# A hybrid attention layer: the output stage's first two row tiles prepared inside the last differential slots, the variance moved off VectorE, and the first loads put between stores

## What is computed

```python
h = _rmsnorm(x, g_pre[layer])
proj = h @ w_in[layer]
...
y_sb = _stick_breaking(...).reshape(b, s_len, SB_WIDTH) * jax.nn.silu(sb_g)
# differential attention: two softmaxes per head over key chunks <= the query's chunk
p = jax.nn.softmax(jnp.where(allowed, sc, -jnp.inf), axis=-1)
a = p[:, :, 0] - lam * p[:, :, 1]
o = einsum('bhqk,bkhe->bqhe', a, v)
y_df = _rmsnorm(o, g_subln) * (1.0 - lambda_init) * jax.nn.silu(df_g)
...
y_m = softmax(mq @ mk) @ mv * jax.nn.silu(m_g)
y = jnp.concatenate([y_sb, y_df, y_m], axis=-1) @ w_out[layer]
x = x + _rmsnorm(y, g_post[layer])
```

## Time and profile before

| | us |
|---|---|
| median of 3 runs (lowest, highest) | 1971.78 (1969.61, 1973.33) |
| the profiled execution, its own time | 1971.71 |
| its span in the trace | 1969.9 |
| PE busy | 1837.9 (93%) |
| DVE busy | 1299.6 (66%) |
| ACT busy | 1076.0 (55%) |
| POOL busy | 606.9 (31%) |

### The profile page before, as it was taken

One profiled execution on the slowest core, in us unless ns is written; L12 is line 12 of the kernel. 1 busy time (PEld: TensorE's weight loads), 2 busy tenths in 40 slices (PEclk: granted clock), 3 DMA queues, 4 the chain that ended last, 5 costly groups with the idle time before them and its releaser, 6 DMA issues.

```text
span 1969.9 us, 34242 instructions
## 1 busy us (share of the span) xinstructions
PE 1837.9 (93%) x11552; PEld 1549.6 (79%) x11552; DVE 1299.6 (66%) x2657; ACT 1076.0 (55%) x2378; POOL 606.9 (31%) x545
## 2 busy tenths in 40 slices
PE   6999999899999999999999999999788999979998
PEld 6999999778787878787777787777566666658886
DVE  7704888577777777777777764344677878753554
ACT  6421112266666666666666753343588998951221
POOL 0000000044444444444444431112246666650000
PEclk9999999899999999999999899998699999999999
DMA  7423213100000101010101013324601432025542
GB/s 223 107 70 112 69 64 118 49 6 13 20 19 13 24 8 25 7 27 5 27 5 27 6 38 115 106 90 133 134 1 40 82 76 44 9 97 203 176 144 86
DMA packets 121841, 129.10 MB, mean 66 GB/s; under 512 B 81937, under 2 KB 94993, under 8 KB 120465
## 3 DMA queue, kind: packets, MB, share of 16 engines
q1 hardware_dynamic: 121312, 126.29, 22.4%
q0 software_dynamic: 432, 1.57, 0.3%
HBM read 85.89 MB, written 41.94 MB: 65 GB/s over the span
## 4 chain that ended last, share of the span: by engine, by line
PE 70%; DVE 14%; issue 6%; ACT 6%; DMA 2%; POOL 1%; SPq 1%; DVEq 0%; ACTq 0%; POOLq 0%
PE ps L685 9%; PE ps L671 6%; PE ps L639 6%; PE ps L640 5%; PE ps L641 5%; DVE small L1541 4%; PE ps L622 3%; PE ps L624 3%; PE ps L623 3%; PE ps L908 3%; PE ps L909 3%; PE ps L910 3%; PE ps L659 3%; PE ps L660 3%; PE ps L859 2%
## 5 line engine op out<-in xcount | busy, mean ns | idle before, releaser
L1664 POOL TENSOR_TENSOR ring_r<-ring,sp_hi 128x512 fp32r<-128x512 f32 (+1 forms) x320 | 359.6, 1124 | 437.5 <-DVE sp_hi L1423 437.5
L685 PEld LDWEIGHTS ps<-v,ring 128*128 128x128 f32 x2176 | 290.0, 196 | 62.8 <-issue 27.4
L685 PE MATMUL ps<-v,ring 128*128 128x65 f32 x2176 | 292.5, 275 | 20.2 <-ACT ring L1070 12.4
L1058 ACT ACTIVATE ring<-ps 128x512 f32<-128x512 f32 (+1 forms) x320 | 170.5, 533 | 218.7 <-PE ps L660 127.6
L1420 DVE SCALAR_TENSOR_TENSOR ring<-ring,ps 128x512 f32<-128x512 f32 (+1 forms) x320 | 192.1, 600 | 44.4 <-ACT ring L1063 41.8
L622 PE MATMUL ps<-w_hl,ht_hi 128*128 128x256 f32 x768 | 213.6, 278 | 0.7 <-DVE w_hl L1268 0.6
L1690 POOL TENSOR_TENSOR p<-p 128x1024 f32<-128x1024 f32 (+4 forms) x96 | 164.7, 1727 | 159.3 <-ACT p L1180 159.0
L623 PE MATMUL ps<-w_hl,ht_hi 128*128 128x256 f32 x768 | 213.3, 278 | 0.0
L624 PE MATMUL ps<-w_hl,ht_lo 128*128 128x256 f32 x768 | 213.3, 278 | 0.0
L639 PE MATMUL ps<-ht_hi,w_hl 128*128 128x512 f32 x448 | 199.6, 446 | 5.2 <-DVE sb_s L1450 4.2
L1541 DVE TENSOR_REDUCE small<-ps 128x1 f32<-128x1024 f32 (+4 forms) x192 | 168.7, 906 | 46.6 <-PE ps L817 26.1
(11 more groups left out here) (202 smaller groups left out, 3897.7 us busy)
## 6 DMA issues: line engine op xcount, KB each, us to landing
xb<-in_x SPq DMA_DIRECT2D x16, 512.0 KB, 3.9
gate_scr<-ring SPq DMA_DIRECT2D x64, 128.0 KB, 1.8
cs<-rot_scr SPq DMA_DIRECT2D x32, 256.0 KB, 3.9
gb<-gate_scr SPq DMA_DIRECT2D x16, 512.0 KB, 3.8
yb<-y_scr SPq DMA_DIRECT2D x16, 512.0 KB, 4.7
xr<-in_x SPq DMA_DIRECT2D x16, 512.0 KB, 4.3
out_y<-ob SPq DMA_DIRECT2D x16, 512.0 KB, 2.9
w_raw<-in_w_narrow SPq DMA_DIRECT2D x15, 512.0 KB, 3.7
```

The lines of the kernel that those rows point to most:

```text
L685: mm = pe.matmul(ps[:, 4 + i % 2, j * (HD + 1):(j + 1) * (HD + 1)], ring[:, 4 + i % 2, j * P:(j + 1) * P], v1[:, kb, :], start=True, stop= ...
L1664: nc.gpsimd.tensor_tensor(ring_r[:, i % 4, j0 * P:], ring[:, i % 4, j0 * P:], sp_hi[:, i % 4, j0 * P:].bitcast(F32), ALU.subtract).then_in ...
```

## The change

Four things are changed.

1. **Variance without VectorE.** `df_variance` keeps only the sum. ScalarE takes Ln of sum/64 + eps directly (scale and a bias column `eps_col`, one more memset at the start), and GpSimd makes the variance for its Newton step itself, as the first instruction of `df_norm`. VectorE's sum now waits until GpSimd and ScalarE have read the sum of the block before.
2. **First two row tiles inside the last slots.** Gates of tiles 0 to 3 are loaded in slot 29, the rows in slot 31. VectorE gates tiles 0, 1 and 2 at the end of slots 32, 33 and 35; TensorE transposes tiles 0 and 1 in slots 33 and 34; `out_hi` and `out_lo` of both stand at the end of slots 33 and 34. The products follow directly behind the loop.
3. **Residual rows and `g_post`** are loaded in slot 35, ahead of the last block's store.
4. **First differential loads between stores.** Head 0's values are loaded in slot 27, and the four parts of its queries and keys in slots 28, 29, 30 and 31, each behind that slot's store of the memory stage.

```diff
-                    load_qk(0)
-                    load_df_v(0)
+                if 3 <= slot - X_SLOT[-1] < 7:
+                    load_qk(0, ((0, 2 * DQ), (0, 0), (1, 2 * DQ), (2, 0))[slot - X_SLOT[-1] - 3])
...
-                if s == N_SL:
+                if s == N_SL - 3:
+                    for i in range(4):
+                        load_gate(i)
+                if s == N_SL - 1:
                     for i in range(4):
                         load_y(i)
+                if s == N_SL + 3:
+                    sp.wait_ge(df_z, N_SL * UNITS)
+                    for u in range(2):
+                        load_xr(u)
+                    sp.wait_ge(df_o, N_SL * N_GR)
+                    sp.dma_start(gpost_b[:], g_post.broadcast_to((P, D))).then_inc(gpost_in, 16)
...
+                if s == N_SL + 1:
+                    pe.wait_ge(df_e, N_SL * UNITS)
+                if s in (N_SL + 1, N_SL + 2):
+                    out_transposes(s - N_SL - 1)
                 df_scores(s, 5)
...
-            pe.wait_ge(df_ob, N_SL // 2)
-            out_transposes(0)
-            out_transposes(1)
             pe.wait_ge(wo_lo_ok, DC)
             for i in range(SB):
+                if i == 1:
+                    pe.wait_ge(df_ob, N_SL // 2)
                 out_products(i)
...
-                rsqrt_of(df_tmp(4, 4), df_tmp(8, 4), df_tmp(12, 4), df_var, s // 2 + 1, df_ln, df_y0)
+                b = s // 2
+                act.wait_ge(df_ss, b + 1)
+                if b:
+                    act.wait_ge(df_nr, 4 * b)
+                nc.scalar.activation(df_tmp(8, 4), df_tmp(0, 4), ACT.Ln, scale=1.0 / HD, bias=eps_col).then_inc(df_ln, 1)
+                act.wait_ge(df_ln, b + 1)
+                nc.scalar.activation(df_tmp(12, 4), df_tmp(8, 4), ACT.Exp, scale=-0.5).then_inc(df_y0, 1)
...
                 df_exp(s, 5)
+                if s in (N_SL + 1, N_SL + 2):
+                    out_hi(s - N_SL - 1)
...
                 dve.wait_ge(df_sq, b + 1)
+                if b:
+                    dve.wait_ge(df_var, b)
+                    dve.wait_ge(df_ln, b)
                 nc.vector.tensor_reduce(ss, osq[:], AXX, ALU.add).then_inc(df_ss, 1)
-                dve.wait_ge(df_ss, b + 1)
-                if b:
-                    dve.wait_ge(df_nr, 4 * b)
-                nc.vector.tensor_scalar(var, ss, 1.0 / HD, EPS, ALU.mult, ALU.add).then_inc(df_var, 1)
...
                 df_rows(s - 4)
+                if s in (N_SL, N_SL + 1, N_SL + 3):
+                    out_gate((N_SL, N_SL + 1, N_SL + 3).index(s))
+                if s in (N_SL + 1, N_SL + 2):
+                    out_lo(s - N_SL - 1)
...
+                pool.wait_ge(df_ss, b + 1)
+                nc.gpsimd.tensor_scalar(var, df_tmp(0, 4), 1.0 / HD, EPS, ALU.mult, ALU.add).then_inc(df_var, 1)
+                pool.wait_ge(df_var, b + 1)
                 pool.wait_ge(df_y0, b + 1)
-                pool.wait_ge(df_var, b + 1)
```

More of the change, by code:

```diff
@@ L447, in store_qk, with load_qk @@
                 sp.dma_start(qk_scr[h, 1, :, cols], lo_tmp[:, f % 2, :].bitcast(F32)).then_inc(qk_out[f % 2], 16)
-            def load_qk(h):
+            def load_qk(h, only=None):
                 u, half = h % 2, S // 2
                 for part, dst, row, first in ((0, df_k, 2 * DQ, 0), (0, df_q, 0, half), (1, df_k, 2 * DQ, half), (2, df_q, 0, 0)):
+                    if only not in (None, (part, row)):
+                        continue
                     cols = slice(first, first + half)
@@ L481, in _ @@
                         store_qk(f)
+                if slot == X_SLOT[-1] + 2:
+                    load_df_v(0)
                 if slot == X_SLOT[-1] + 3:
@@ L496, in _, with load_xr @@
             load_qk(1)
+            def load_xr(i):
+                if i >= 2:
+                    sp.wait_ge(o_fin, i - 1)
+                sp.dma_start(xr[:, i % 2, :], x[OUT_ROWS[i] * P:(OUT_ROWS[i] + 1) * P, :]).then_inc(o_xr[i % 2], 16)
             def load_wo(k):
@@ L501, in load_wo, with load_gate @@
                 sp.dma_start(w_raw[:, (k % 2) * D:(k % 2 + 1) * D], w_out[k * P:(k + 1) * P, :]).then_inc(wo_in[k % 2], 16)
+            def load_gate(i):
+                if i == 0:
+                    sp.wait_ge(df_z, (DF_H - 1) * 8 * UNITS)
+                row = OUT_ROWS[i]
+                sp.dma_start(gb[:, i % 4, :], gate_scr[row * P:(row + 1) * P, :]).then_inc(o_in[i % 4], 16)
             def load_y(i):
@@ L553, in store @@
                 sp.dma_start(out[OUT_ROWS[i] * P:(OUT_ROWS[i] + 1) * P, :], ob[:, i % 2, :]).then_inc(o_out[i % 2], 16)
-            for u in range(2):
-                load_xr(u)
             for i in range(SB):
@@ L911, in out_products @@
                     mm.then_inc(o_ps, 1)
-            pe.wait_ge(df_ob, N_SL // 2)
-            out_transposes(0)
-            out_transposes(1)
+            for s in range(N_SL + 4):
+                df_scores(s, 0)
+                df_scores(s, 1)
+                df_turn(s - 2, 0)
+                df_values((s - 2) * N_GR + 0 - 1)
+                df_scores(s, 2)
+                df_turn(s - 2, 1)
+                df_values((s - 2) * N_GR + 1 - 1)
+                df_scores(s, 3)
+                df_turn(s - 2, 2)
+                df_scores(s, 4)
+                df_values((s - 2) * N_GR + 2 - 1)
+                df_turn(s - 2, 3)
+                df_values((s - 2) * N_GR + 3 - 1)
+                if s == N_SL + 1:
+                    pe.wait_ge(df_e, N_SL * UNITS)
+                if s in (N_SL + 1, N_SL + 2):
+                    out_transposes(s - N_SL - 1)
+                df_scores(s, 5)
+                df_turn(s - 2, 4)
+                df_values((s - 2) * N_GR + 4 - 1)
+                df_turn_back(s - 4)
             pe.wait_ge(wo_lo_ok, DC)
             for i in range(SB):
+                if i == 1:
+                    pe.wait_ge(df_ob, N_SL // 2)
                 out_products(i)
@@ L1217, in _, with out_hi @@
                 act.wait_ge(qk_out[u], 32 * len(X_D) // 2)
+            def out_hi(i):
+                u = i % 2
+                act.wait_ge(o_tps, i + 1)
+                if i >= 2:
+                    act.wait_ge(o_ps, 2 * (i - 2) + 2)
+                for g in range(2):
+                    nc.scalar.activation(yt_hi[:, u, 4 * g:4 * g + 4, :],
+                                         ps[:, 2 * u + g, :].rearrange("p (c s) -> p c s", c=4), ACT.Copy).then_inc(o_thi, 1)
             for s in range(N_SL + 6):
@@ L1588, in df_variance, with out_gate, out_lo @@
                 b = s // 2
-                ss, var = df_tmp(0, 4), df_tmp(4, 4)
+                ss = df_tmp(0, 4)
                 dve.wait_ge(df_sq, b + 1)
+                if b:
+                    dve.wait_ge(df_var, b)
+                    dve.wait_ge(df_ln, b)
                 nc.vector.tensor_reduce(ss, osq[:], AXX, ALU.add).then_inc(df_ss, 1)
-                dve.wait_ge(df_ss, b + 1)
-                if b:
-                    dve.wait_ge(df_nr, 4 * b)
-                nc.vector.tensor_scalar(var, ss, 1.0 / HD, EPS, ALU.mult, ALU.add).then_inc(df_var, 1)
             for u in range(4):
                 dve.wait_ge(m_yout[u], 16 * N_MT // 4)
+            def out_gate(i):
+                dve.wait_ge(o_in[i % 4], 32 * (i // 4 + 1))
+                nc.vector.tensor_tensor(yb[:, i % 4, :], yb[:, i % 4, :], gb[:, i % 4, :], ALU.mult).then_inc(o_yg, 1)
+            def out_lo(i):
+                u = i % 2
+                for g in range(2):
+                    dve.wait_ge(o_thi, 2 * i + g + 1)
+                    nc.vector.tensor_tensor(yt_lo[:, u, 4 * g:4 * g + 4, :], ps[:, 2 * u + g, :].rearrange("p (c s) -> p c s", c=4),
+                                            yt_hi[:, u, 4 * g:4 * g + 4, :].bitcast(F32), ALU.subtract).then_inc(o_tlo, 1)
             for s in range(N_SL + 6):
@@ L1638, in out_norm @@
                 nc.vector.tensor_tensor(ob[:, u, :], ob[:, u, :], xr[:, u, :], ALU.add).then_inc(o_fin, 1)
-            for i in range(3):
-                out_gate(i)
-            for i in range(2):
-                out_lo(i)
             dve.wait_ge(gpost_in, 16)
```

50 lines of the change are left out of this document (4 added, 46 removed).

## The result

| | before | changed |
|---|---|---|
| median, us (runs; lowest, highest) | 1972.55 (4; 1969.61, 1975.54) | 1941.65 (4; 1940.73, 1943.59) |
| ratio, 95% interval | | 0.9845 (0.9827, 0.9862) |
| span of the profiled execution | 1969.9 | 1941.8 |

The account below looks back on a forecast made before the run. Idle time at the output stage's start, behind VectorE's variance in the slot pairs, and at a store wait ending the memory stage was to be filled: 15 + 0.8 + 12.8 = 28.6 off 1971.7, called 1943; range 1937 to 1953.

Parts of the forecast that it names:

- A, the variance: Differential stage: taking the stalled variance off VectorE removes TensorE's and ScalarE's waits behind it; 15 us.
- The walk through slot 29: Differential stage, one slot followed engine by engine without the stall: 16.1 us in all, 15 taken.
- ScalarE as the tighter engine: Slot pairs: ScalarE runs gapless, so TensorE gets 1.1 of its 1.5 us; sign: exponential waits of 0.3 to 0.4.
- The ceiling: Slot pairs: at about 19.9 us each with TensorE busy 19.6, no more than 17.8 us can be won.
- GpSimd's instruction as hidden: Differential stage: GpSimd's added variance, 0.4 us with its wait, is hidden; uncovered it would be 6 us.
- GpSimd late for its block: Rival, differential stage: GpSimd slips, VectorE's sum and the next slots queue behind it; 1972 us and rising; chance 0.02.
- B, the loads: End of the memory stage: first loads between stores free the store VectorE waits for; first scores 0.8 us earlier.
- C, the first product: Start of the output stage: first product at 1762.1 instead of 1772.05, 9.95 us won after 1.9 of delays.
- The port: Start of the output stage: GpSimd's last add waits for VectorE's first gating at their shared port; 0.9 us charged.
- The order at the port: Rival, start of the output stage: GpSimd's add goes first and the gating waits, 1.8 us for 0.9; 1944; chance 0.05.
- The clock: Output stage, tile 0: TensorE keeps the granted clock of 1.00, its 48 products take 10.95 instead of 13.75; 2.8 us.
- the slower rival: Differential stage: GpSimd late, VectorE's sum waiting, 1972 us and rising, chance 0.02; late row loads were a separate 0.01 case.

Follow-up runs that it names:

- x_act: The changed kernel with two more 128x4 ScalarE instructions behind the root of each block; 1945.04 us, ratio 0.9847.
- x_pe: The changed kernel with three transposes of group 2 made twice in every second slot; 1944.59 us, ratio 0.9840.
- split: The kernel before, with VectorE's variance left there but written as four 128x1 instructions instead of one 128x4; 1954.27 us, ratio 0.9903.
- x_mem: The changed kernel with VectorE's 128x2 negation in the memory stage's last six items written as two 128x1 instructions; 1940.89 us, ratio 0.9841.

## Why the prediction held, and where it didn't

**A, the variance: 15 forecast, 16.2 measured** (sum to turn back, with and without the other parts). The walk through slot 29 gave 16.1; the us taken off for tight hand-overs wasn't needed. Three steps of the reasoning fell all the same. *ScalarE as the tighter engine:* the waits for the exponential of 0.3 to 0.4 that I named as its sign hardly came (0.22 us at 1709.59 is one of the few), and `x_act` and `x_pe` show ScalarE as the one without room in five pairs of 14 only. *The ceiling:* 17.8, worked out from a TensorE that is busy 19.6 of 19.9 us, isn't one, since `split` gained 18.3 on the same stretch; a busy TensorE had room left. *GpSimd's instruction as hidden:* it was priced at 0 because GpSimd is idle 8 of 21 us. It costs 1.6 to 2, in the few slots where a `wo_lo` block stands beside the norm. The rival "GpSimd late for its block" named the right engine, but VectorE's sum was not what waited; TensorE's turn was. So the agreement of 16.1 and 16.2 is luck in part: the stall was worth at least 18.3 and not 16.1, and GpSimd's instruction took back 2 that I had at nothing. The mechanism that held is the stall itself, its 14 places and that the sum doesn't inherit it.

**B, the loads: 0.8 forecast, 0.74 measured,** 0.73 alone.

**C, the first product: 9.95 forecast, 10.55 measured.** I counted 1.9 us of delays on the path and it was 1.3. The port was over-priced. GpSimd's add took 2.96 us instead of 2.35, as it should behind a gating that had started first, but a turn waits only 0.20 for it, and I had charged 0.9. The order at the port didn't turn. *The clock: 2.8 forecast, 2.79 measured.*

**The sum** was 28.6; by stretches 30.3 without the 0.2 between scores and sum, by the ratio 30.6. The misses, 1.2 in A and 0.6 in C, are both on the careful side. Nothing of the slower rival was seen: the row loads were on time, and VectorE's sum waited for GpSimd only once, 0.80 us at 1740.06, when the copy that TensorE needed next was still 1.8 us away.

**Open:** what bounds the third pair, in which none of the three edits changed anything; what lets VectorE in between the two memsets in one execution and not in another; and what sets the moment at which the clock falls, 6.5 us behind the last projection product in one execution, 10 in another and 20 in `x_mem`, which no edit here explains.

## What to carry to other kernels

Before moving an instruction that stalls, read what runs on GpSimd beside it and try another form in the same place: two or four 128x1 `tensor_scalar` in place of one wide one took 0.2 to 0.34 us together where the wide one was held up for 1.2 to 2.3, and twice for some 6, in both places of this kernel. Price an instruction added to an idle engine in the slots where that engine is fullest, not by its average. At the border of two stages look at the granted clock as well as the waits (6 us lay between an execution at the low level and one at the high level here), and compare executions by stretches between landmarks, not by their spans.
